# A three-layer transformer kernel on one Trainium2 core: the top-k rounds of the sparse attention spread over two attentions, the indexer moved ahead of them, and the forget sums added from a table

## The reference

```python
# moba: logits + T5 bias by distance; with 2 blocks of 256 keys and top 3, every past key is taken
s = q @ k.T * scale + table_t[:, t5_bucket(t - s)];  s = where(t - s >= 0, s, NEG_BIG)
# forgetting attention: c = cumsum(log_sigmoid(f_logit + b)) for each head
logits = q @ k.T * scale + c[t] - c[s];  p = softmax(where(s <= t, logits, NEG_BIG))
# dsa (sparse): indexer score, top 128 keys for each query, softmax over them with T5 bias
isc = relu(einsum('bqhe,bke->bqhk', q_idx, k_idx))      # 8 index heads of 32
isc = einsum('bqh,bqhk->bqk', w_idx, isc)
_, idx = top_k(where(admissible, isc, -inf), 128)
logits = q @ k[idx] * scale + table_t[:, t5_bucket(dist)]
```

## Time and profile before

| | us |
|---|---|
| median of 3 runs | 3468.81 (3468.24 to 3469.7) |
| the profiled execution | 3477.65 |
| its span | 3476.0 |

### The profile page before, as it was taken

How to read it: one execution, slowest core, us unless ns; L and a number is a source line. 1 busy time by engine, 2 the same in 40 slices (tenths; PEclk the granted TensorE clock), 3 DMA queues, 4 the chain that set the end, 5 groups by cost and what they waited for, 6 DMA issues and landing times.

```text
span 3476.0 us, 38938 instructions
## 1 busy us (share of the span) xinstructions
PE 3314.2 (95%) x14989; PEld 2620.7 (75%) x14989; DVE 1472.1 (42%) x2225; ACT 739.9 (21%) x1332; POOL 2231.6 (64%) x2554
## 2 busy tenths in 40 slices
PE   7989999999999999998899999999999889999998
PEld 5777566678887888877667888778887776788886
DVE  2222553257742752157554331343313765533214
ACT  3223223322211111032231110121102232311003
POOL 3444135679987887764238777787777433577776
PEclk9999679999999999999899999999999999999999
DMA  4211011223332333231113333233323211133332
GB/s 128 61 46 54 25 37 55 67 85 97 97 97 88 109 97 97 91 79 48 30 41 97 94 93 101 86 97 97 97 92 91 55 45 46 56 99 94 97 97 79
DMA packets 469297, 273.26 MB, mean 79 GB/s; under 512 B 20926, under 2 KB 466288, under 8 KB 469112
## 3 DMA queue, kind: packets, MB, share of 16 engines
q1 hardware_dynamic: 468056, 268.65, 26.3%
q10 hardware_dynamic: 1056, 2.12, 0.2%
HBM read 268.58 MB, written 2.12 MB: 78 GB/s over the span
## 4 chain that ended last, share of the span: by engine, by line
PE 87%; DVE 6%; POOL 3%; ACT 2%; issue 1%; SPq 0%; DMA 0%; DVEq 0%; POOLq 0%; ACTq 0%
PE bank L651 16%; PE bank L652 16%; PE bank L656 16%; PE bank L1016 6%; PE bank L1010 6%; PE bank L1011 6%; DVE arena L1907 2%; POOL wl L616 2%; PE bank L894 1%; PE bank L837 1%; PE bank L683 1%; PE bank L1169 1%; PE bank L827 1%; PE bank L685 1%; PE bank L684 1%; PE bank L746 1%
## 5 line engine op out<-in xcount | busy, mean ns | idle before, releaser
L616 POOL TENSOR_TENSOR wl<-raw,wh 128x256 fp32r<-128x256 f32 x2040 | 1669.8, 849 | 42.6
L611 POOL TENSOR_SCALAR wh<-raw 128x1024 fp32r<-128x1024 f32 x510 | 564.3, 1106 | 1179.1 <-PE bank L656 510.2
L651 PE MATMUL bank<-xh,wh 128*128 128x512 f32 x1568 | 633.2, 404 | 0.0
L652 PE MATMUL bank<-xl,wh 128*128 128x512 f32 x1568 | 622.7, 397 | 0.0
L1907 DVE TENSOR_TENSOR arena<-arena 128x512 f32<-128x512 f32 (+2 forms) x474 | 403.0, 867 | 105.9 <-ACT arena L1744 45.0
L656 PE MATMUL bank<-xh,wl 128*128 128x512 f32 x1568 | 390.2, 389 | 0.0
L1907 DVE TENSOR_TENSOR arena<-bank,nrm 128x512 f32<-128x512 f32 x236 | 152.0, 686 | 533.1 <-PE bank L656 532.9
L651 PEld LDWEIGHTS bank<-xh,wh 128*128 128x128 f32 x1568 | 303.7, 194 | 66.4 <-issue 2.2
L652 PEld LDWEIGHTS bank<-xl,wh 128*128 128x128 f32 x1568 | 302.9, 193 | 65.2 <-issue 2.2
L656 PEld LDWEIGHTS bank<-xh,wl 128*128 128x128 f32 x1568 | 294.3, 188 | 61.2
L651 PE MATMUL bank<-arena_rounded,wh 128*128 128x512 f32 x816 | 323.5, 396 | 0.0
(11 more groups left out here) (317 smaller groups left out, 4553.0 us busy)
## 6 DMA issues: line engine op xcount, KB each, us to landing
raw<-in_ffn_w_gate SPq DMA_DIRECT2D x176, 256.0 KB, 3.3
raw<-in_ffn_w_up SPq DMA_DIRECT2D x176, 256.0 KB, 3.2
raw<-in_ffn_w_down SPq DMA_DIRECT2D x176, 256.0 KB, 3.0
raw<-in_w_in SPq DMA_DIRECT2D x158, 256.0 KB, 3.3
raw<-in_w_up SPq DMA_DIRECT2D x88, 256.0 KB, 3.3
raw<-in_w_gate SPq DMA_DIRECT2D x64, 256.0 KB, 3.2
raw<-in_w_out SPq DMA_DIRECT2D x48, 256.0 KB, 3.2
raw<-in_w_down SPq DMA_DIRECT2D x44, 256.0 KB, 2.9
```

Of the source, the lines that this page charges most:

```text
L611: pool.tensor_scalar(wh[:, s, :], raw[:, s, :], 1.0, 0.0, ALU.mult, ALU.add).then_inc(split, 1)
L616: ins = pool.tensor_tensor(wl[:, s, c], raw[:, s, c], wh[:, s, c].bitcast(F32), ALU.subtract)
L651: pe.matmul(psum, cols(wh, i), xhi, start=(i == 0), stop=False)
L652: pe.matmul(psum, cols(wh, i), xlo, start=False, stop=False)
```

## The change

- `SB_BEHIND`: `dsf` and `dst` are now projected behind unit 11 of `sb`, `fxq` and `fxk` behind units 12 to 15; the DMAs of their pieces follow the same order. ACT copies `dsf` and `dst` out behind unit 12. `fxv` leaves `sb`.
- The indexer stands ahead of `mb`. Four heads, which lie on four groups of 32 partitions, go to four banks with one semaphore increment; between the six such groups PE does a sixth of the projection `fxv` each. The next group waits until all four banks have been read.
- The 48 top-k rounds are split: two behind each unit of `mb`, one behind each unit of `fx`.
- The forget sums: c[t] is dropped (it is one number for a softmax row), and -c[s] is made as a table 128x512 for each head by one product of 4 rows (`decay_table`), which ACT copies over the bias tables of `mb`; DVE adds it in the instruction that takes the maximum, as in `mb`.
- The part of the distance table for s > t is filled with -1e30 by a memset, so `mb` needs no diagonal mask product, nor does the first query block of `ds`; a small product and its copy at the start go.

```diff
-SB_BEHIND = ("mbq", "mbk", "mbv", "fxq", "fxk", "fxv", "dsq", "ix")
+SB_BEHIND = ("mbq", "mbk", "mbv", "dsq", "ix", "dst", "fxq", "fxk")
+ROUNDS = [(2 * u, 2 * u + 1) for u in range(16)] + [(32 + u,) for u in range(16)]
...
         def behind(names, key, u):
 
             name = names[u // 2]
-            if name in ("mbv", "fxv", "hi", "zv", "rv"):
+            if name in ("mbv", "dst"):
                 if u % 2:
-                    gemm_tm((name, *key), xk)
+                    gemm_tm((name, *key), xk, ("dsf",) if name == "dst" else None)
             else:
                 gemm_half((name, *key), xk, u % 2)
...
-        def qk(o, q, kk, i):
-            pe.matmul(o[:, 0:(i + 1) * P], q[:, i * P:i * P + P], kk[:, 0:(i + 1) * P], start=True, stop=False)
+        def qk(o, q, kk, i, more=True):
+            return pe.matmul(o[:, 0:(i + 1) * P], q[:, i * P:i * P + P], kk[:, 0:(i + 1) * P], start=True,
+                             stop=not more)
...
         def score_mb(o, hh, i):
-            qk(o, heads(mbq, hh), heads(mbk, hh), i)
-            return diagonal(o, i, "causal")
+            return qk(o, heads(mbq, hh), heads(mbk, hh), i, False)
 
         def score_fx(o, hh, i):
             qk(o, heads(fxq, hh), heads(fxk, hh), i)
-            one = pick[0:NH, :].rearrange("p (g h q) -> p g h q", g=2, h=NH)
-
-            for j in range(i + 1):
-                pe.matmul(o[:, j * P:j * P + P], cum[0:NH, i * P:i * P + P], one[:, 0, hh, :], start=False, stop=False)
-            pe.matmul(o[:, 0:(i + 1) * P], one[:, 1, hh, :], cum[0:NH, 0:(i + 1) * P], start=False, stop=False)
             return diagonal(o, i, "causal")
 
...
             r = slice(hh % 2 * HD, hh % 2 * HD + HD)
-            pe.matmul(o[:, 0:(i + 1) * P], dsq[r, hh // 2, i * P:i * P + P], dsk[r, 0:(i + 1) * P],
-                      start=True, stop=False)
+            ins = pe.matmul(o[:, 0:(i + 1) * P], dsq[r, hh // 2, i * P:i * P + P], dsk[r, 0:(i + 1) * P],
+                            start=True, stop=(i == 0))
             if i == 0:
-                return diagonal(o, i, "causal")
+                return ins
             return pe.matmul(o[:, 0:(i + 1) * P], ident, sel[:, i - 1, 0:(i + 1) * P], start=False, stop=True)
...
-        gemm_tm(("dst",), xk, ("dsf",))
...
+        def decay_table(hh):
+
+            s = slab_start(("fxt", hh))
+            pe.wait_ge(*T.at("cum"))
+            one = pick[0:NH, :].rearrange("p (g h q) -> p g h q", g=2, h=NH)
+            pe.matmul(bank[2 * s][:, :], one[:, 1, hh, :], cum[0:NH, :], start=True, stop=True)\
+                .then_inc(*T.up("gemm", "fxt", hh))
+
         def gates_behind(b):
-            return lambda u: gate_piece(b, u // 4, u % 4) if u % 4 < 3 else None
+            def between(u):
+                if u % 4 < 3:
+                    gate_piece(b, u // 4, u % 4)
+                elif b == 0 and u >= 7:
+                    decay_table(u // 4 - 1)
+                elif b == 1 and u == 3:
+                    decay_table(3)
+            return between
 
         pe.wait_ge(*T.at("o", "sb", 1))
         pe.wait_ge(*T.at("evac", "dst"))
         pe.wait_ge(*T.at("evac", "ix"))
+        values = grains_tm(("fxv",), xk)
+        places = (SC[0], SC[1], PT, OB)
+        for b in range(6):
+            i, g = b // 2 + 1, b % 2
+            if b:
+                pe.wait_ge(*T.at("ix_used", 4 * b - 1))
+            for m in range(4):
+                r = slice(32 * m, 32 * m + 32)
+                ins = pe.matmul(places[m][:, 0:(i + 1) * P], ixq[r, g, i * P:i * P + P], ixk[r, 0:(i + 1) * P],
+                                start=True, stop=True)
+            ins.then_inc(*T.up("ix_score", b))
+            next(values)
+        pe.wait_ge(*T.at("ix_used", 23))
         attention("mb", score_mb, lambda hh, j: mbv[:, j, hh * HD:hh * HD + HD], 1, gates_behind(0))
...
-        n = 0
-        for i in range(1, TT):
-            for hh in range(8):
-                if n >= 2:
-                    pe.wait_ge(*T.at("ix_used", n - 2))
-                r = slice(hh % 4 * 32, hh % 4 * 32 + 32)
-                pe.matmul(SC[n % 2][:, 0:(i + 1) * P], ixq[r, hh // 4, i * P:i * P + P], ixk[r, 0:(i + 1) * P],
-                          start=True, stop=True).then_inc(*T.up("ix_score", n))
-                n += 1
-        pe.wait_ge(*T.at("cum"))
-        for u in (n - 2, n - 1):
-            pe.wait_ge(*T.at("ix_used", u))
         attention("fx", score_fx, lambda hh, j: fxv[:, j, hh * HD:hh * HD + HD], 1, gates_behind(1))
         pe.wait_ge(*T.at("o", "fx", 1))
...
         def gates_behind(b):
             def between(u):
                 if u % 4 == 2:
                     gate_on(b, u // 4, gates[:, u // 4 % 2 * 2:, :])
+                if b == 0 and u in (8, 12):
+                    decay_table(u // 4 - 2)
+                if b == 1 and u in (0, 4):
+                    decay_table(2 + u // 4)
             return between
+
+        def latent_keys_in():
+            s = evac_start(("dsf",))
+            for a in range(2):
...
+                if u == 12:
+                    latent_keys_in()
...
+        for n in range(24):
+            m, w = n % 4, (n // 8 + 2) * P
+            if m == 0:
+                act.wait_ge(*A.at("ix_score", n // 4))
+            if n >= 2:
+                act.wait_ge(*A.at("ix_added", n - 2))
+            act.activation(soft[:, n % 2, 0:w], (SC[0], SC[1], PT, OB)[m][:, 0:w], ACT.Relu)\
+                .then_inc(*A.up("ix_used", n))
         attention("mb", 1, True, gates_behind(0), 1)
-        n = 0
-        for i in range(1, TT):
-            for hh in range(8):
-                act.wait_ge(*A.at("ix_score", n))
-                if n >= 2:
-                    act.wait_ge(*A.at("ix_added", n - 2))
-                act.activation(soft[:, n % 2, 0:(i + 1) * P], SC[n % 2][:, 0:(i + 1) * P], ACT.Relu)\
-                    .then_inc(*A.up("ix_used", n))
-                n += 1
-        attention("fx", 1, False, gates_behind(1), 2)
+        attention("fx", 1, True, gates_behind(1), 2)
...
-                    v.tensor_tensor_reduce(pr[:, u % 2, 0:n], SC[u % 2][:, 0:n], bias[:, table + hh, S - n:S], 1.0, GONE,
+                    if tag == "fx" and i == 0:
+                        v.wait_ge(*V.at("evac", "fxt", hh))
+                    v.tensor_tensor_reduce(pr[:, u % 2, 0:n], SC[u % 2][:, 0:n], table(hh, n), 1.0, GONE,
                                            ALU.add, ALU.max, stat[:, u % 2, 0:1])\
                         .then_inc(*V.up("score_used", tag, u))
...
+        v.memset(t5_rev[0:8, 512:640], NEG).then_inc(*V.up("t5_masked"))
...
-            if u and u % 2 == 0:
+            if u and u % 2 == 0 and SB_BEHIND[u // 2 - 1] != "dst":
                 w_in_out(SB_BEHIND[u // 2 - 1])
...
-        attention("mb", 1, 0, gates_behind(0))
-        branch_rest(1)
-
...
+        w_in_out("fxv")
+
         def largest_behind(u):
 
-
-            for n in range(3 * u, 3 * u + 3):
+            for n in ROUNDS[u]:
...
-            gates_behind(1)(u)
-
-        attention("fx", 1, None, largest_behind)
+
+        def largest_and_gates(b):
+            def between(u):
+                largest_behind(16 * b + u)
+                gates_behind(b)(u)
+            return between
+
+        def by_distance(first):
+            return lambda hh, n: bias[:, first + hh, S - n:S]
+
+        attention("mb", 1, by_distance(0), largest_and_gates(0))
+        branch_rest(1)
+        attention("fx", 1, lambda hh, n: bias[:, hh, 0:n], largest_and_gates(1))
         branch_rest(2)
 
         def late_behind(u):
@@ -2128,7 +2158,7 @@
                 if unit_of(3 * g + 2) + 1 == u:
                     gate_branch(2, g, gates[:, g % 2 * 2:, :], soft)
 
-        attention("ds", 1, 4, late_behind)
+        attention("ds", 1, by_distance(4), late_behind)
         branch_rest(3)
         for g in range(DC // 2):
             gate_branch(3, g, late_gates[:, 2 * g:, :], soft)
```

More of the change, by code:

```diff
@@ L495, in _ @@
         w = k["w_in"][0]
-        for name in ("sbq", "sbk", "sbv", "mbq", "mbk", "mbv", "fxq", "fxk", "fxv", "dsq", "ixq"):
+        for name in ("sbq", "sbk", "sbv", "mbq", "mbk", "mbv", "dsq", "ixq"):
             slab(w, A_COLS[name])
@@ L500, in _ @@
         piece(some(w, A_COLS["ixk"], 40, 0), some(w, A_COLS["fxf"], NH, HD))
+        for name in ("fxq", "fxk", "fxv"):
+            slab(w, A_COLS[name])
         gate_w, branch_w = k["w_gate"][0], k["w_branch"][0]
@@ L2053, in w_in_out @@
         def w_in_out(name):
[L2055 removed]
+            dst = dict(mbq=mbq, mbk=mbk, mbv=mbv, fxv=fxv, fxq=fxq, fxk=fxk, dsq=dsq, ix=ixq)[name]
             s = evac_start((name,))
```

37 lines of the change are left out of this document (17 added, 20 removed).

## The result

The changed kernel takes 3415.6 us (median of 4 runs, 3411.9 to 3416.89) beside 3468.77 (3468.24 to 3469.7, 4 runs): 53.2 us less, ratio 0.9845, 95% interval 0.9828 to 0.9862. The prediction said 3411.0 in a range of 3396 to 3432. The profiled execution took 3416.89 us for a span of 3415.6; that of before took 3477.65 for 3476.0. So between the two profiles the gain is 60.4 us of span, between the medians 53.2. That difference turns out to be the main lesson of this case.

The account below looks back on a forecast made before the run. PE and what PE waits for bound the kernel. 20.3 - 0.2 - 30.7 - 48.5 - 0.7 + 2.0 = -57.8 us: 3419.9 from the profiled 3477.65, 3411.0 from the median; range 3396 to 3432.

Parts of the forecast that it names:

- The end of `sb`: `sb` grows by 10.9 us of projection, 3.7 waiting for ACT's copy and 2.6 of clock, ending at 242.9 instead of 225.72.
- Forget sums and indexer: Between `sb` and `mb`: first relu at 251.1, adds paced by DVE until 274.1, `mb` begins at 277.3, +20.3 us.
- Rival B: Indexer: the four row groups run one after the other, +12.0 us, 3423, at low clock twice that; chance 0.06.
- C: Top-k rounds are half open: half of some 60 us of DVE on the path, +30, 3441 us; chance 0.05.
- D: DVE's queue becomes the chain in both attentions; slower, 3523 us if all its work is open; chance 0.02.
- The link: Between `mb` and `fx`: the old 33.94 us of indexer and start of `fx` become 3.2, so -30.7.
- `fx`: Stage becomes like `mb` with another table: 94.67 + 3.8 + 1.35 = 99.8 us against 148.29, -48.5.
- The rest: `ds` saves three masks, 0.7 us; one more half-speed stretch somewhere adds 2.0; all behind the first block is untouched.
- cross-check: `fx` saving by what goes: 4-row products 26.4 us and waits 7.6 - 3.8, together 30.2; the remaining 18 from the clock.
- A: Clock stays at half through the indexer (+7.5 us) and falls at heads of `fx` (0.88, 8 us): 3426.5; chance 0.12.
- E: More gained: no wait lowers the clock, `mb` and `fx` start fast, 3399 us; 3395 with early `dsf` copies; chance 0.11.
- F: Change doesn't do what it says: a pair of banks holds each gate slab until DVE's branch; chance 0.02.

Follow-up runs that it names:

- second profile: The kernel before, unchanged, profiled and timed once more: median 3469.5 us over 10 runs, profiled execution 3469.86 us with a span of 3467.3.

## Why the prediction was right, and where it was off

**The bound.** PE, and what PE waits for: right. Each experiment that moved the time did so through PE's own instructions, through a wait of PE, or through the clock that follows it.

**The end of `sb`.** The wait of PE for ACT's copy of `dsf` was put at 3.7 and is 3.3; its cost in the clock at 2.6 and is 1.8. `sb` was to end at 242.9; its last product of values starts at 242.66 and takes 1.09, so 243.75. There is some luck in that: against before as it ran first `sb` grew by 18.0, against its second profile by 15.7 (its end there is 228.06), where 17.2 was forecast and the terms as measured give 10.9 + 3.3 + 1.8 = 16.0.

**Forget sums and indexer.** First relu predicted at 251.1, measured 250.65: two of DVE's instructions were quicker than before, 5.0 us for the chain instead of 6.12. DVE done with the adds predicted at 274.1, measured 275.5 (the last at 274.85, 0.69 long). The start of `mb` predicted at 277.3, measured 278.77. The assumption under it, that four row groups cost as much as one, holds: 1.14 beside 1.12 us. Its far bound, 12 us, is near what the serial form costs in the trace, 13.6. Rival B is out. The Trainium skill (TensorE: Matmul & The Clock Gate, Part 3) measured a gain of 3.07 of 4 for 512 columns; these groups agree, with 2.8 at 256 columns, 3.1 at 384 and an estimated 3.2 at 512. But a group was 0.71 to 1.14 us long at full clock, as the rows for one product had it, so the 1.3 us that the prediction would have added by it (1.2, if 5 x 0.8 x 0.30 is meant) were not there to add.

**`mb`.** 94.5 predicted, 93.64 measured. The masks were worth 3.4 there, and are 2.8 (from its start to that of `fx`); two rounds a unit cost 1.2 at most (the one wait for DVE of 0.37 is there without them as well). The 3.2 for the three table products is a term that no run confirms: taking them out made the stage no shorter. So the total is nearer than its terms. C and D, the rivals in which DVE becomes the chain, are out.

**The link.** 3.2 predicted, 3.17 measured.

**`fx`.** 99.8 predicted, 102.11 measured; the four waits are 0.5 to 1.5, where 1 to 2 was said. What is over, 2.3 us, is the size of the clock's part: the same instructions took 99.32 us at 0.98 with `dsf` out early. The row at 471.88 shows DVE idle 4.02 us until ACT's gate for the last branch, and that branch with its rest takes until 477.55, so this chain of ACT and DVE sets the first maximum of `ds`, and PE waits 2.6 behind it.

**The rest.** Predicted at 0.7 less and 2.0 more for a half-speed stretch. Measured from the first maximum of `ds`: 2937.9 against 2942.1, and 2940.4 in the second profile of before, so 2.5 to 4.2 less.

**The step that was off** is "I make the sum against the former and take the difference over to the median". As a sum against the profiled execution it was 3419.9, and the profiled execution of after took 3416.9. But the 8.84 us by which the profile of before stood above the median were no constant of profiling. They lay in `fx`, the stage that the change shortens most, as 9.45 us of low clock that the second execution of before did not have (the stages ahead and behind differed by 2.35 and 1.75, nearly cancelling). The term "-48.5" was nearly right against the first (-46.2), and took 9.45 too much from a median that goes with an `fx` of 138.84: from there 99.8 is -39.0, and the same sum gives 3420.4. Measured against the second profile of before, that stage lost 36.7. So the point forecast was 4.6 too low because one term was 9.45 too large and the others together 4.8 too cautious: the rest of the program -2.5 where +1.3 was forecast, `mb` with the link -31.9 where -30.9 was, the start of `mb` +19.4 (278.77 against 259.34) where +20.3 was, against them `fx` 2.3 too short; 1.5 more lie between the spans and the medians. The cross-check in the prediction had the sign of it: its products and waits came to 30.2, and 18 us more were put to the clock. With the typical stage it would have been 9. And the 26.4 in it were no pure work: at full clock these products are 19.5, so the clock's share was larger than the cross-check has it. In the run with the products back it was half.

**The rivals A and E.** A's 0.88 in `fx` didn't come (0.95), nor its pace by PE in the indexer, though the clock there was 0.86. E's idea, that ACT's copies of `dsf` can be met early, was right as an edit: it gave 8.1, where E had 4 for it, and 3402.0 together with the early forget sums, which E did not have; its 3395 to 3399 was not reached. F, a pair of banks held too long, is out: from the start of `mb` to that of `ds` no gate slab of PE waits for a bank.

## What to carry to other kernels

Before a profiled execution is laid under a forecast, compare it with the runs: where it stands apart by more than their spread, find the stage in which it does (a second profile, or the granted clock by stage), and don't carry the difference over if the change touches that stage.
A small wait of a busy PE costs more than itself: 1.8 us on top of 3.3, 2.8 on top of 4.6. Both could be had by writing an engine's instruction a few places earlier, without any change of work.
Filler for DVE goes where PE is bound and DVE idle, spread thin: one round a unit was hidden, two cost 1.2 us at most, three cost 8.2 and 5.5, in either attention.
Busy time of PE that was read in a stretch of low clock is not work: take the granted clock of the same stretch beside it (what took 2.64 us at 0.72 took 1.95 at full clock).

## What the runs showed of the hardware

Four fp32 products of 32 rows on four row groups take as long as one of 64 rows (1.14 and 1.12 us at 512 columns). On one row group the same four took 2.8 times as long at 256 columns, 3.1 at 384 and 3.4 to 3.6 at 512 (the last at a clock of 0.95 and 0.91), with full-size projections between the groups.
One program can take 9.45 us more or less in one stage of 139 us, with the same instructions and waits, by the granted clock alone (0.78 or 0.84), while the stage just ahead agrees to 0.2 us.
Products of 4 rows are as dear as full ones: at full clock four of 128 columns took 1.00 us from start to start, 0.25 each, beside 0.24 for the mask product of 128 rows, and one of 512 columns 0.95 beside 1.05 for one of 64 rows (390.07 to 391.12).
The clock is lower in a stage with many of them (0.85, and 0.83 with the rounds) than without (0.95, and 0.94 with the rounds). It does not go with PE's waits for DVE within the stage: they were 2.5 us at 0.85 and 10.0 at 0.94. What about these products lowers it was not tested.
